# First gate panel of a branch ahead of its stage border, and an earlier split of the mixed sum

## What is computed

```python
pl = _split_cols(u @ w_in + b_in)                 # u: normalised, modulated input
att_l  = attention over context and latent keys   # 16 heads of 64
conv_l = p[3] * _dwconv(p[4] * p[5], w)           # short gated convolution
dn_l   = bidirectional gated delta rule, chunked  # 8 heads of 128
gates = jax.nn.sigmoid(gz)                        # gz = the last 3 * 1024 columns of u @ w_in + b_in
m = (gates[..., :D_MODEL] * (att @ w_br[0])
     + gates[..., D_MODEL:2 * D_MODEL] * (conv @ w_br[1])
     + gates[..., 2 * D_MODEL:] * (dn @ w_br[2]))
out = m @ w_out
h = h + ml[:, 5, None] * out
```

## Time and profile before

| | us |
|---|---|
| median of 3 runs | 3353.94 (3353.17 to 3354.42) |
| the profiled execution, its own time | 3349.25 |
| its span, first to last instruction | 3347.5 |
| VectorE busy, share of the span | 52% |
| ScalarE busy, share of the span | 42% |
| mean granted TensorE clock | 0.982 |
| moved by DMA | 363.43 MB, mean 109 GB/s |

### The profile page before, as it was taken

The page is one execution under the profiler, slowest core; times in us unless marked ns, Lnnn a source line. Parts: engine busy times, 40 slices in busy tenths (PEclk is TensorE's granted clock), DMA queues, the critical chain, the costliest instruction groups (busy, mean ns, idle before and its releaser), DMA issues.

```text
span 3347.5 us, 51456 instructions
## 1 busy us (share of the span) xinstructions
PE 3190.4 (95%) x18766; PEld 2651.3 (79%) x18766; DVE 1740.0 (52%) x3164; ACT 1406.5 (42%) x2189; POOL 124.1 (4%) x120
## 2 busy tenths in 40 slices
PE   7999989999989899999999999999999998899898
PEld 4777768888877578777788867777788888699898
DVE  4333357777634823434333343334677775856555
ACT  4222256565434722224222242223655654654544
POOL 0000010111000000000000000000000000000000
PEclk9999999999999999999999999999899999999999
DMA  7443421111122043222432243434111113144454
GB/s 285 149 152 127 159 87 64 38 56 44 45 82 82 1 145 120 88 94 97 162 104 97 97 148 132 169 132 155 60 50 50 56 51 117 54 147 164 155 183 145
DMA packets 101261, 363.43 MB, mean 109 GB/s; under 512 B 11153, under 2 KB 12817, under 8 KB 101009
## 3 DMA queue, kind: packets, MB, share of 16 engines
q1 hardware_dynamic: 98384, 353.02, 30.9%
q10 hardware_dynamic: 2752, 8.72, 0.7%
HBM read 360.58 MB, written 1.11 MB: 108 GB/s over the span
## 4 chain that ended last, share of the span: by engine, by line
PE 85%; DVE 7%; ACT 4%; issue 3%; DMA 1%; SPq 0%; DVEq 0%; POOL 0%; POOLq 0%; ACTq 0%
PE bank L1662 67%; PE bank L1919 3%; PE bank L1917 2%; DVE wlo L1013 2%; PE bank L1687 2%; ACT whi L490 1%; PE bank L1970 1%; ACT scr L932 1%; PE bank L1978 1%; DVE h L1113 1%; PE bank L1988 1%; PE bank L1990 1%; PE bank L2125 1%; PE bank L2148 1%; PE bank L1960 1%
## 5 line engine op out<-in xcount | busy, mean ns | idle before, releaser
L1662 PE MATMUL bank<-uh,whi 128*128 128x512 f32 (+1 forms) x3008 | 1118.0, 372 | 52.9 <-ACTq L890 17.0
L1662 PE MATMUL bank<-ul,whi 128*128 128x512 f32 (+1 forms) x3008 | 1084.5, 361 | 0.0
L1662 PE MATMUL bank<-uh,wlo 128*128 128x512 f32 (+1 forms) x3008 | 1082.8, 360 | 0.5 <-DVE scr L1403 0.3
L490 ACT ACTIVATE whi<-raw 128x1024 fp32r<-128x1024 f32 x520 | 548.2, 1056 | 1209.3 <-PE bank L1662 1208.9
L1013 DVE TENSOR_TENSOR wlo<-raw,whi 128x1024 fp32r<-128x1024 f32 x520 | 642.4, 1235 | 790.5 <-ACT whi L490 789.2
L1662 PEld LDWEIGHTS bank<-uh,whi 128*128 128x128 f32 x3008 | 578.2, 192 | 160.5 <-issue 63.8
L1662 PEld LDWEIGHTS bank<-uh,wlo 128*128 128x128 f32 x3008 | 576.5, 192 | 81.8 <-DVE scr L1403 1.6
L1662 PEld LDWEIGHTS bank<-ul,whi 128*128 128x128 f32 x3008 | 578.7, 192 | 69.8 <-issue 2.2
L1662 PE MATMUL bank<-bh,whi 128*128 128x512 f32 (+1 forms) x1088 | 387.9, 357 | 1.1 <-DVE h L1113 0.8
L1662 PE MATMUL bank<-bl,whi 128*128 128x512 f32 (+1 forms) x1088 | 384.5, 353 | 0.0
L1662 PE MATMUL bank<-bh,wlo 128*128 128x512 f32 (+1 forms) x1088 | 384.4, 353 | 0.0
(11 more groups left out here) (247 smaller groups left out, 3041.3 us busy)
## 6 DMA issues: line engine op xcount, KB each, us to landing
raw<-stream SPq DMA_DIRECT2D x524, 512.0 KB, 3.3
ada_raw<-stream SPq DMA_DIRECT2D x131, 512.0 KB, 5.2
gc_row<-gc_rows ACTq DMA_DIRECT2D x16, 512.0 KB, 3.6
h<-h_in SPq DMA_DIRECT2D x1, 2048.0 KB, 10.9
m<-stream SPq DMA_DIRECT2D x4, 512.0 KB, 12.4
cst<-consts SPq DMA_DIRECT2D x1, 1104.0 KB, 12.5
scr<-stream SPq DMA_DIRECT2D x2, 512.0 KB, 16.2
out<-m SPq DMA_DIRECT2D x8, 128.0 KB, 1.8
```

The lines of the kernel that those rows point to most:

```text
L490: act.activation(whi[:, j, :], raw[:, j, :], ACT.Copy).then_inc(hi_ready, 1)
L1662: last = mm(bank[j][:, c0:T], w(t, a), x[:, t, c0:T], start=n == 0, stop=n == 3 * kts - 1)
```

## The change

It has three parts.

1. **Attention to its branch.** VectorE releases banks 0 and 1 when head pair 6 is done, and banks 2 and 3 at the end. TensorE issues the first 6 matmuls of the attention branch's first gate panel between the last transposes and the last value product, and the other 18 behind that product. The branch no longer issues that panel, and waits for the last `att_low` ahead of its second panel.
2. **Conv to its branch.** The branch issues its first gate panel first, and waits for conv's last output behind it. For both, the first block of branches 1 and 2 is written out ahead of the loop.
3. **Split of the mixed sum.** ScalarE starts its copies after the last gate panel and once tiles 0 to 5 are added, with waits of their own for tiles 6 and 7. VectorE does the subtractions of tiles 0 to 6 (`m_low`) inside the last step of the conv branch, behind the split of weight panel 2 and ahead of the last multiply and add; that of tile 7 stays in `project_out`. The last step is taken out of VectorE's loop for this.

```diff
@@ -963,9 +963,11 @@
     def project_out(l):
         B0, G0 = P[("out", l)]
         c0 = CTX if l == DEPTH - 1 else 0
-        act.wait_ge(panel_done, 4 * B0)
-        have(act, pair_done[1], G0)
+        act.wait_ge(panel_done, 4 * B0 - 1)
+        have(act, pair_done[1], G0 - 1)
         for t in range(KT):
+            if t >= KT - 2:
+                have(act, pair_done[t % 2], G0)
             act.activation(uh[:, t, c0:T], m3[:, t, c0:T], ACT.Copy).then_inc(C["mh_ready"], 1)
         last_residual(B0, G0, 3 * l + 2)
 
@@ -1445,6 +1447,12 @@
         head(l, DNH, False)
         split(B0 + DNH + 1, 3)
 
+    def m_low(l, t):
+
+        c0 = CTX if l == DEPTH - 1 else 0
+        dve.wait_ge(C["mh_ready"], 8 * l + t + 1)
+        dve.tensor_tensor(ul[:, t, c0:T], m3[:, t, c0:T], uh[:, t, c0:T].bitcast(f32), ALU.subtract).then_inc(C["mx_ready"], 1)
+
     def branch(l, r):
         B0, G0 = P[("br", l, r)]
         c0 = CTX if l == DEPTH - 1 else 0
@@ -1452,7 +1460,7 @@
 
         g0, rides = P[("rides", l, "br")] if r == 1 else (0, 0)
 
-        def step(i):
+        def step(i, last=False):
             B = B0 + i
             for k in range(2):
                 if r == 0 and isinstance(i, int):
@@ -1464,6 +1472,9 @@
                                             bank[6 + j][:, :]).then_inc(A["a_vtok"], 1)
                     qk_norm(10 * l + k, l * NVL + V_KG, kT[:, k, :], kT[:, k, :], 0)
                 split(B + 1, 2 * k)
+                if last and k:
+                    for t in range(KT - 1):
+                        m_low(l, t)
                 dve.wait_ge(panel_done, 4 * B + 2 * k + 2)
                 dve.wait_ge(C["br_gate"], n0 + 2 * i + k + 1)
                 mt = m3[:, ds(2 * i + k, 1), c0:T].rearrange("p a t -> p (a t)")
@@ -1483,8 +1494,10 @@
         else:
             if r == 0:
                 step(0)
-            with steps.loop(1 if r == 0 else 0, 4, 0 if r == 0 else 2) as i:
+            with steps.loop(1 if r == 0 else 0, 3 if r == 2 else 4, 0 if r == 0 else 2) as i:
                 step(i)
+            if r == 2:
+                step(3, True)
         for k in range(2):
             have(dve, pair_done[k], G0 + 4)
 
@@ -1521,6 +1534,9 @@
                 dve.wait_ge(A["att_hi"], 8 * l + j + 1)
                 dve.tensor_tensor(bl[:, j, c0:T], bank[j % 2][:, c0:T], bh[:, j, c0:T].bitcast(f32),
                                   ALU.subtract).then_inc(A["att_low"], 1)
+                if j == 6:
+                    dve.wait_ge(A["att_low"], 8 * l + 7)
+                    dve.sem_inc(pair_done[0], 2)
 
         for n, (j, kind) in enumerate(pairs):
             w = 1 if kind else 2
@@ -1545,8 +1561,7 @@
         for n in range(N - 3, N):
             out_low(n)
         dve.wait_ge(A["att_low"], 8 * (l + 1))
-        for k in range(2):
-            dve.sem_inc(pair_done[k], 2)
+        dve.sem_inc(pair_done[1], 2)
 
     def conv(l):
         B0, G0 = P[("conv", l)]
@@ -1609,9 +1624,7 @@
     def project_out(l):
         B0, G0 = P[("out", l)]
         c0 = CTX if l == DEPTH - 1 else 0
-        for t in range(KT):
-            dve.wait_ge(C["mh_ready"], 8 * l + t + 1)
-            dve.tensor_tensor(ul[:, t, c0:T], m3[:, t, c0:T], uh[:, t, c0:T].bitcast(f32), ALU.subtract).then_inc(C["mx_ready"], 1)
+        m_low(l, KT - 1)
         gates(l, 1)
         last_residual(B0, G0, 3 * l + 2, c0)
         have(dve, pair_done[0], G0 + 2)
@@ -2041,13 +2054,18 @@
         B0, G0 = P[("br", l, r)]
         c0 = CTX if l == DEPTH - 1 else 0
         g0, rides = P[("rides", l, "br")] if r == 1 else (0, 0)
-        for s, n in ready:
-            have(pe, s, n)
+        if r == 0:
+            for s, n in ready:
+                have(pe, s, n)
         if rides:
             for i in range(4):
                 for j in range(4):
-                    pair_free(G0 + i, j)
-                    panel(B0 + i, j, *((uh, ul) if j % 2 == 0 else (bh, bl)), c0)
+                    if (i, j) == (0, 1):
+                        for s, n in ready:
+                            have(pe, s, n)
+                    if (i, j) != (0, 0):
+                        pair_free(G0 + i, j)
+                        panel(B0 + i, j, *((uh, ul) if j % 2 == 0 else (bh, bl)), c0)
                     if j % 2 == 0:
                         ada_pair(g0 + i, j // 2)
                 ada_turn(g0 + i)
@@ -2063,7 +2081,15 @@
                     qk_sum(10 * l + j // 2, 0)
                 else:
                     qk_swap(10 * l + j // 2, kT[:, j // 2, :])
-        with pe.Fori(1 if r == 0 else 0, 4) as i:
+        else:
+            for j in range(4):
+                if j == 1:
+                    for s, n in ready:
+                        have(pe, s, n)
+                if (r, j) != (1, 0):
+                    pair_free(G0, j)
+                    panel(B0, j, *((uh, ul) if j % 2 == 0 else (bh, bl)), c0)
+        with pe.Fori(1, 4) as i:
             for j in range(4):
                 pair_free(G0 + i, j)
                 panel(B0 + i, j, *((uh, ul) if j % 2 == 0 else (bh, bl)), c0)
@@ -2149,14 +2175,19 @@
                                   PT[:, a, at:at + 128], start=kt == 0, stop=kt == (3 if kind else 1))
             last.then_inc(A["s_pv"], 1)
 
+        B1, G1 = P[("br", l, 1)]
         scores(0)
         for n in range(N + 1):
             if n + 1 < N:
                 scores(n + 1)
+            if n == N:
+                pair_free(G1, 0)
+                panel(B1, 0, uh, ul, c0, hi=6)
             if n:
                 pv(n - 1)
             if n < N:
                 turn(n)
+        panel(B1, 0, uh, ul, c0, lo=6)
 
     def conv(l):
         B0, G0 = P[("conv", l)]
@@ -2186,7 +2217,7 @@
         heads(l, 3 * l + 1)
         branch(l, 0, [(pair_done[1], P[("kv", l)][1] + 1)])
         attention(l)
-        branch(l, 1, [(pair_done[0], P[("q", l)][1] + 2), (pair_done[1], P[("q", l)][1] + 2)])
+        branch(l, 1, [(A["att_low"], 8 * l + 7)])
         conv(l)
         branch(l, 2, [(pair_done[1], P[("conv", l)][1] + 6)])
         project_out(l)
```

## The result

| | before | after |
|---|---|---|
| median, us | 3354.18 (3353.17 to 3354.57) | 3333.91 (3331.96 to 3334.45) |
| profiled execution, us | 3349.25 | 3334.18 |
| its span, us | 3347.5 | 3332.4 |

The change makes the kernel faster by 20.3 us at the median; the ratio is 0.9945 [0.9933, 0.9957], so 0.55%. The forecast was 3337.6 us, in a range of 3333 to 3344. The two profiled executions are only 15.1 us apart. The next lines show where these went; the experiments show where the other five are.

A forecast was written before the change was run, and what follows sets the result against it. TensorE, busy 95% of the span, was taken as the bound, so only its idle pieces could give time: 2.7 + 2.3 + 6.7 + 5.3 + 0.4 - 1.1 = 16.3 us off 3353.94 gives 3337.6 us, range 3333 to 3344.

The forecast's parts named there:

- Border 1: End of attention: six gate matmuls ahead of the last value product, 18 behind; gain 2.7 us in layer 0, 2.3 in layer 1.
- the cover of the last subtraction: End of attention, layer 0: the last head's copy and subtraction, 1.4 us, now lie beside the 4.1 us of 18 matmuls.
- Border 2: Conv to its branch: first gate panel runs at once; gain 6.7 us in layer 0, 5.3 in layer 1.
- conv's end is bound by VectorE's chain, which does not move: Conv to branch, layer 1: the 2.89 us panel fits into the 4.55 us gap; second panel starts at 3060.65, not 3065.93.
- Border 3: Split of the mixed sum, branch to projection: gain 0.4 us in layer 0, loss 1.1 us in layer 1.
- ScalarE's weight split held the copies: Mixed sum: ScalarE's new wait frees nothing, as its split of weight panel 3 waits for the branch's last panel.
- VectorE's queue makes the loss of layer 1: Mixed sum, layer 1: eighth subtraction stands behind last multiply, add and weight split, ending 3115.8; loss 1.1 us.
- the step on the clock: Conv to branch, layer 1: 5.3 us gain holds if the clock stays up across the remaining 1.7 us of gap.
- the clock falls anyway: Rival, chance 0.12: short gaps at border 2 of layer 1 and border 3 leave half clock, costing 6.0 us; 3343.6.
- the weight stream: Rival, chance 0.05: weight loads set layer 1, so its 2.3 + 5.3 us would be given back; 3345.2.
- straight code: Rival, chance 0.03: twelve panels written out starve TensorE; at 2 us lost a panel, 24 us slower, 3361.6.
- does not do what it says: Rival, chance 0.04: border 2's first panel still waits for the same low part; 12.0 us would go, 3349.6.

The follow-up runs named there:

- Part 1 alone: Only the first attention gate panel issued around the last value product, against the kernel before: 3347.62 us, ratio 0.9985 [0.9976, 0.9994].
- part 3 alone: Only the split of the mixed sum changed, against the kernel before: 3354.31 us, ratio 1.0002 [0.9993, 1.0011].
- the sixth kernel: Whole change, with the eighth subtraction moved ahead of VectorE's split of weight panel 3: 3333.24 us, ratio to before 0.9944 [0.9931, 0.9958].
- part 2 alone: Only the conv branch's first gate panel put ahead of the wait for conv's last output, against the kernel before: 3341.62 us, ratio 0.9963 [0.9950, 0.9977].

## Why the prediction held, and where it did not

**Border 1.** Forecast 2.7 and 2.3 us, read from the profiles 2.51 and 2.31. Part 1 alone gave 0.15%, 5.0 us. The order of queues and the cover of the last subtraction were as stated. The 0.2 us that layer 0 fell short are the changes between kinds of matmuls: the 6 took 1.56 us (1177.10 to 1178.66) where the sum had 1.4, and the 18 took 4.31 (1179.69 to 1184.00) where it had 4.1.

**Border 2.** Forecast 6.7 and 5.3, read 6.79 and 5.53. In layer 0 the panel filled the whole gap, in layer 1 the second panel started right when conv's low part let it go. The step "conv's end is bound by VectorE's chain, which does not move" held: conv's last subtraction starts 6.63 us after ScalarE's weight split at conv's end, in both (3059.89 less 3053.26 before; 3049.20 less 3042.57 after).

**Border 3.** Forecast a gain of 0.4 us in layer 0 and a loss of 1.1 in layer 1; read 0.57 and 0.88. That ScalarE's weight split held the copies is shown from both sides: part 3 alone is no change, and with the copies ahead of the split the kernel gains 6.7 us. That VectorE's queue makes the loss of layer 1 is shown only in part: its eighth subtraction came as late as stated, but with the queue eased (the sixth kernel) the low clock, which the sum did not have there, held the panel nearly as long, so the near hit of 0.88 is in part luck. The forecast of layer 0 was too small for most executions: with 5 slow matmuls in the old border it is 0.57 us, in the four other profiles without part 3, with 7 to 13, it is 0.8 to 2.1, since the end of VectorE's queue does not depend on the clock.

**What failed** is the step on the clock, though it cost the sum little: "if the clock stays up across what is left of the gap (1.7 us, less than the 2.83 us after which it was still up)". At border 2 it did stay up. But the rule behind it, that a gap shorter than one that left the clock up does so too, does not hold. (Nor did the window in the earlier trace rows show it: that window is the gap itself, and only the 0.36 us row behind it said that the clock was up.) The 2.00 us gap ahead of the projection of layer 1 had 17 slow matmuls behind it in the changed kernel, and 11 to 18 in all four profiles of kernels with that gap, while the longer 2.83 us gap had none in four of five. The rival "the clock falls anyway" was right about this place, and wrong about its price: it counted 2.3 us, and the low clock added almost nothing, since VectorE's eighth subtraction came as late as the slow matmuls did. Where nothing else was as late, it did cost: 7.33 us instead of 6.00 in part 1 alone, 1.3 us.

**The size.** The sum was 16.3 us, the landmarks give 16.8, the medians 18.7 and 20.3. The term that was too small is the low clock behind the old gaps. I took it from one profile, where 6 matmuls in a row were slow at the conv border of layer 0 and none behind attention. In the three other profiles with the old conv border it was 11 to 13, 1.0 to 1.4 us more at 0.20 us each, and in two of them another 5 to 6 behind attention in layer 0, again 1.0 to 1.2 us. At the conv border of layer 1 it was the other way round: the first profile had the most slow matmuls of the four, and by the others border 2 gives 4.5 to 5.5 us there. Counted in whole stretches (from the last transposes to the first update of h, both layers added), the two profiles of before take 520.3 and 523.1 us and both profiles of the changed kernel 503.5: a gain of 16.8 or 19.6 us, around the 18.7 of the medians. The rest lies in stretches that the change does not touch: from the first update of h in layer 0 to the last transposes of layer 1, the ten profiles differ by up to 4.6 us. The clock goes with it: in the three shortest (1418.2 to 1419.8 us) it was at half for 41 to 48 us, in the seven others (1420.3 to 1422.8) for 55 us each. What sets it in one execution stays open; no run was made for it.

The rivals of the weight stream, of straight code and of a change that "does not do what it says" did not show: the blocks written out have no gap but the 0.32 and 0.82 us above, and both of these end with an output of conv.

## What to carry to other kernels

A wait at a stage border often covers work that does not need it: issue first what reads old data only, and place the wait at its first real reader. Before moving a wait, read what stands ahead of it in the same queue: here the wait on the mixed sum was not the one that held ScalarE, a weight split one instruction earlier was, and copies issued ahead of that split were worth 6.7 us (the place of the eighth subtraction, moved with them, gave 0.3 in its own run, less than the noise), where moving the wait was worth nothing. And when a short idle time is priced, take the low clock behind it from several profiles, not from one.

## What the runs showed of the hardware

- A gap of the same length does not always have the low clock behind it. The 1.5 to 1.7 us gap at the end of attention occurs eight times in the four profiles that have it (before twice, part 2 alone, part 3 alone; two layers each): three times 5 to 15 matmuls behind it were slow, five times none. The granted clock of 15 us around it was 0.89 or 1.00 with the same instructions.
- A longer gap was not the worse one: 2.00 us ahead of the projection of layer 1 was followed by slow matmuls in four profiles of four, 2.83 us at the same place in one of five. What TensorE did before was the same, a full branch at clock 1.00. Why is open.
- At the low level matmuls of 512 columns start 0.427 us apart and those of 256 columns 0.213, at the full level 0.227 and 0.120. So each slow one costs 0.20 or 0.09 us, if TensorE is what ends the stretch.
- Weights and inputs of an open accumulation can be interrupted: 6 matmuls into bank 0, 16 of another kind into bank 1, then 18 into bank 0. The first matmul behind each change of kind took 0.31 to 0.34 us to the next start instead of 0.23.
